# Spreading the tokens' inverse roots by two transfers through device memory instead of eight matmuls

## The reference

```python
def rms_norm(x, gain=None):
    y = x * lax.rsqrt(jnp.mean(x * x, axis=-1, keepdims=True) + EPS)
    ...
def modulate(h, shift, scale):
    return h * (1 + scale[:, None, :]) + shift[:, None, :]

for i in range(DEPTH):
    mod = cond @ mod_w[i] + mod_b[i]
    sh1, sc1, g1, sh2, sc2, g2, sh3, sc3, g3 = jnp.split(mod, 9, axis=-1)
    h = modulate(rms_norm(x), sh1, sc1)
    x = x + 0.5 * g1[:, None, :] * swiglu(h, ffn1_w_gu[i], ffn1_w_down[i])
    h = modulate(rms_norm(x), sh2, sc2)
    ...                                   # y = dsa_mixer(h) or fox_mixer(h)
    x = x + g2[:, None, :] * y
    h = modulate(rms_norm(x), sh3, sc3)
    x = x + 0.5 * g3[:, None, :] * swiglu(h, ffn2_w_gu[i], ffn2_w_down[i])
    x = rms_norm(x, post_gain[i])
```

## Time and profile before

| | |
|---|---|
| median of 3 runs | 2023.62 us (2021.04 to 2023.71) |
| the profiled execution | 2023.55 us, its span 2021.7 us |
| TensorE busy | 1986.2 us (98%), 9174 matmuls |
| VectorE busy | 1109.7 us (55%) |
| ScalarE busy | 726.7 us (36%) |
| GpSimd busy | 193.4 us (10%) |
| mean granted clock of TensorE | 0.993 |
| transfers | 253.97 MB, mean 126 GB/s |

### The profile page before, as it was taken

How to read it: one execution, slowest core, us unless ns; L and a number is a source line. 1 busy time by engine, 2 the same in 40 slices (tenths; PEclk the granted TensorE clock), 3 DMA queues, 4 the chain that set the end, 5 groups by cost and what they waited for, 6 DMA issues and landing times.

```text
span 2021.7 us, 23587 instructions
## 1 busy us (share of the span) xinstructions
PE 1986.2 (98%) x9174; PEld 1645.4 (81%) x9174; DVE 1109.7 (55%) x1705; ACT 726.7 (36%) x1066; POOL 193.4 (10%) x221
## 2 busy tenths in 40 slices
PE   6999999999999999999999999999999999999997
PEld 4888888888888888888888888877888888888886
DVE  7665553788757655636863553475454573333334
ACT  5222312554644222225322222345555442222223
POOL 3110000026600100000110100000000000000000
PEclk9999999999999999999999999999999999999998
DMA  8665542322025655623553632222221122323221
GB/s 318 239 214 180 184 156 88 100 87 74 22 98 194 216 172 194 189 77 108 188 190 104 205 125 83 94 84 64 73 72 54 63 94 104 104 83 108 81 87 57
DMA packets 72014, 253.97 MB, mean 126 GB/s; under 512 B 8025, under 2 KB 8153, under 8 KB 71938
## 3 DMA queue, kind: packets, MB, share of 16 engines
q1 hardware_dynamic: 53280, 185.62, 28.0%
q0 software_dynamic: 18512, 67.26, 10.0%
q10 hardware_dynamic: 146, 0.09, 0.0%
HBM read 250.70 MB, written 2.10 MB: 125 GB/s over the span
## 4 chain that ended last, share of the span: by engine, by line
PE 76%; issue 19%; DVE 3%; POOL 1%; ACT 1%; DMA 0%; POOLq 0%; SPq 0%; DVEq 0%; ACTq 0%
PE bank L1297 23%; PE bank L1302 23%; PE bank L1298 23%; PE bank L1762 1%; PE bank L1720 1%; PE bank L1361 1%; PE bank L1651 1%; PE bank L1493 1%; PE bank L1495 1%; DVE dve_tmp L876 1%; PE bank L1494 0%; PE bank L1708 0%; DVE wlo L751 0%; PE bank L1626 0%; DVE h_lo L869 0%
## 5 line engine op out<-in xcount | busy, mean ns | idle before, releaser
L1297 PE MATMUL bank<-h_hi,whi 128*128 128x512 f32 x1808 | 712.3, 394 | 6.8 <-DVE wlo L751 4.5
L1298 PE MATMUL bank<-h_hi,wlo 128*128 128x512 f32 x1808 | 706.1, 391 | 0.0
L1302 PE MATMUL bank<-h_lo,whi 128*128 128x512 f32 x1808 | 594.1, 390 | 0.5 <-POOL h_lo L331 0.5
L411 ACT ACTIVATE whi<-wraw 128x1024 fp32r<-128x1024 f32 x338 | 347.1, 1053 | 267.0 <-PE bank L1302 263.9
L751 DVE TENSOR_TENSOR wlo<-wraw,whi 128x1024 fp32r<-128x1024 f32 x324 | 389.2, 1223 | 57.3 <-ACT whi L411 56.5
L1297 PEld LDWEIGHTS bank<-h_hi,whi 128*128 128x128 f32 x1808 | 341.2, 189 | 79.3 <-issue 5.0
L1302 PEld LDWEIGHTS bank<-h_lo,whi 128*128 128x128 f32 x1808 | 340.5, 188 | 73.1 <-POOL h_lo L331 1.2
L1298 PEld LDWEIGHTS bank<-h_hi,wlo 128*128 128x128 f32 x1808 | 341.0, 189 | 68.6
L1297 PE MATMUL bank<-hid_hi,whi 128*128 128x512 f32 x832 | 324.3, 390 | 0.0
L1302 PE MATMUL bank<-hid_lo,whi 128*128 128x512 f32 x832 | 323.7, 389 | 0.0
L1298 PE MATMUL bank<-hid_hi,wlo 128*128 128x512 f32 x832 | 323.7, 389 | 0.0
(11 more groups left out here) (239 smaller groups left out, 1390.1 us busy)
## 6 DMA issues: line engine op xcount, KB each, us to landing
wraw<-in_w_units_dram SPq DMA_DIRECT2D x306, 512.0 KB, 3.5
arena<-in_mod_t_dram POOLq DMA_DIRECT2D x96, 512.0 KB, 4.9
mod_tile<-in_mod_t_dram POOLq DMA_DIRECT2D x32, 512.0 KB, 4.7
wraw<-in_w_units_dram SPq DMA_DIRECT2D x32, 384.0 KB, 3.4
arena<-in_mod_t_dram SPq DMA_DIRECT2D x12, 512.0 KB, 7.9
xT<-in_xt_dram SPq DMA_DIRECT2D x8, 256.0 KB, 4.5
out_dram<-xT SPq DMA_DIRECT2D x8, 256.0 KB, 2.3
mod_tile<-in_mod_t_dram SPq DMA_DIRECT2D x2, 512.0 KB, 9.5
```

The lines of the kernel that those rows point to most:

```text
L411: act.activation(whi[:, s % RING, :, :], wraw[:, s % RING, :, :], ACT.Copy).then_inc(hi_ready, 1)
L1297: pe.matmul(dst, whi[:, w, k, :], hi_, start=first, stop=False)
L1298: pe.matmul(dst, wlo[:, w, k, :], hi_, start=False, stop=False)
L1302: return pe.matmul(dst, whi[:, s % RING, k, :], lo_, start=False, stop=last)
```

## The change

In norms 1, 2, 5 and 6 the root no longer goes through TensorE and a bank. ScalarE issues a transfer of `rstd` (128 partitions x 4 numbers, 16 bytes each) to a row of 512 numbers in device memory, waits until it has landed, and issues a second one that reads this row for each of the 128 partitions into `ssum`. VectorE waits for the second. The row has the order of partition first and block second, so token b * 128 + p lies at place 4 p + b. The VectorE instructions that read `ssum` view it as 4 blocks of 128 numbers with a step of four (`from_row`), and their other operands as 4 blocks of 128 neighbours (`by_block`). The splits of the root and the eight matmuls go; the counts that other waits use (`ROOTS_BEFORE`, `rb_kept`, `rb_ready`, `root_ready`) follow.

```diff
+        BY_DMA = [1, 2, 5, 6]
+        def by_block(ap):
+            return ap.rearrange("q (b p) -> q b p", b=NB)
+        def from_row(ap):
+            return ap.rearrange("q (p b) -> q b p", b=NB)
...
+        norm_roots = nc.dram_tensor("norm_roots", (len(BY_DMA), SEQ), F32).ap()
...
             def round_h(st, s):
-                act.wait_ge(rb_ready, RB_BEFORE[v])
-                act.activation(ssum[:, :], bank[RB], ACT.Copy).then_inc(rb_kept, 1)
+                if st in BY_DMA:
+                    n, j = BY_DMA.index(st), NORM_JOB[st]
+                    act.wait_ge(rstd_ready, j + 1)
+                    act.dma_start(norm_roots[n, :].rearrange("(p b) -> p b", b=NB), rstd[:, j % 2, 0:NB])\
+                        .then_inc(norm_root_out, 16)
+                    act.wait_ge(norm_root_out, 16 * (n + 1))
+                    act.dma_start(ssum[:, :], norm_roots[n:n + 1, :].broadcast_to([P, SEQ])).then_inc(norm_root_in, 16)
...
             def spread_rstd(st):
                 if st in NORM:
                     lo(LAST_UNIT[st] - 1)
-                split_roots(j, NB)
-                if st in NORM:
                     lo(LAST_UNIT[st])
                 else:
-                    dve.wait_ge(rb_ready, st + 1)
+                    split_roots(j, NB)
+                    dve.wait_ge(rb_ready, 4 if st else 1)
...
             def early_ffn(s):
                 for q in range(2):
-                    dve.tensor_tensor(sq[:, q, :], bank[(s + q) % 4], ssum[:, :], ALU.mult).then_inc(evicted, 1)
+                    ...
+                        dve.tensor_tensor(by_block(sq[:, q, :]), by_block(bank[(s + q) % 4]), from_row(ssum[:, :]),
+                                          ALU.mult).then_inc(evicted, 1)
...
             def norm(st, s, take_early, late=False):
-                dve.wait_ge(rb_kept, v)
+                    dve.wait_ge(norm_root_in, 16 * (BY_DMA.index(st) + 1))
...
-                    dve.scalar_tensor_tensor(out=dve_tmp[:, k % 2, :], in0=xT[:, k, :], scalar=column[:, k:k + 1],
-                                             in1=ssum[:, :], op0=ALU.mult, op1=ALU.mult).then_inc(normed, 1)
+                        dve.scalar_tensor_tensor(out=by_block(dve_tmp[:, k % 2, :]), in0=by_block(xT[:, k, :]),
+                                                 scalar=column[:, k:k + 1], in1=from_row(ssum[:, :]), op0=ALU.mult,
+                                                 op1=ALU.mult).then_inc(normed, 1)
...
             def early(s, st):
-                        if q == 0 and k == 6 and st != 3:
-                            stat_spread(RB, ROOTS_BEFORE[st], NORM_JOB[st])
```

More of the change, by code:

```diff
@@ L225, in build @@
         gained, pool_posted = sem("gained"), sem("pool_posted")
+        norm_root_out, norm_root_in = sem("norm_root_out"), sem("norm_root_in")
         rows_done, rows_kept = sem("rows_done"), sem("rows_kept")
@@ L384, in _ @@
             job(18, 4)
-            pool.wait_ge(rb_kept, len(NORM) + 1)
+            pool.wait_ge(rb_kept, 2)
             pool.wait_ge(gained, KT)
@@ L393, in build @@
         POST_RB = 4
-        ROOTS_BEFORE = [0, 1, 3, 4, 5, 6, 15, 16]
+        ROOTS_BEFORE = {0: 0, 3: 2, 4: 3, 7: 12}
         LAST_UNIT = {st: down + KT + 3 for st, down in (
@@ L432, in round_h @@
                 v, sh, _ = modulation(st)
-                act.wait_ge(rb_ready, RB_BEFORE[v])
-                act.activation(ssum[:, :], bank[RB], ACT.Copy).then_inc(rb_kept, 1)
+                if st in BY_DMA:
[5 more added lines that the diff above has]
+                    act.dma_start(ssum[:, :], norm_roots[n:n + 1, :].broadcast_to([P, SEQ])).then_inc(norm_root_in, 16)
+                else:
+                    act.wait_ge(rb_ready, 2)
+                    act.activation(ssum[:, :], bank[RB], ACT.Copy).then_inc(rb_kept, 1)
                 for k in range(KT):
@@ L732, in _ @@
             ffn(3, 7)
-            act.wait_ge(rb_ready, 9)
+            act.wait_ge(rb_ready, 5)
             act.activation(ssum[:, :], bank[4], ACT.Copy).then_inc(rb_kept, 1)
@@ L842, in early_ffn @@
                 for q in range(2):
-                    dve.tensor_tensor(sq[:, q, :], bank[(s + q) % 4], ssum[:, :], ALU.mult).then_inc(evicted, 1)
+                    if s == FFN_BASE[2]:
+                        dve.tensor_tensor(sq[:, q, :], bank[(s + q) % 4], ssum[:, :], ALU.mult).then_inc(evicted, 1)
+                    else:
+                        dve.tensor_tensor(by_block(sq[:, q, :]), by_block(bank[(s + q) % 4]), from_row(ssum[:, :]),
+                                          ALU.mult).then_inc(evicted, 1)
             def early_dsa(s):
                 early_shift(s)
-                link(dve.tensor_tensor(sq[0:72, 0, :], bank[EARLY_BANK[1][0]][0:72, :], ssum[0:72, :], ALU.mult))
+                link(dve.tensor_tensor(by_block(sq[0:72, 0, :]), by_block(bank[EARLY_BANK[1][0]][0:72, :]),
+                                       from_row(ssum[0:72, :]), ALU.mult))
                 dve.tensor_scalar(ikx[0:72, :], sq[0:72, 0, :], shift_out[0:72, 0:1], None, ALU.add).then_inc(evicted, 1)
-                dve.tensor_tensor(sq[:, 1, :], bank[EARLY_BANK[1][1]], ssum[:, :], ALU.mult).then_inc(early_scaled, 1)
+                dve.tensor_tensor(by_block(sq[:, 1, :]), by_block(bank[EARLY_BANK[1][1]]), from_row(ssum[:, :]), ALU.mult)\
+                    .then_inc(early_scaled, 1)
             def early_fox(s):
                 early_shift(s)
-                link(dve.tensor_tensor(sq[0:HEADS, 0, :], bank[EARLY_BANK[4][0]][0:HEADS, :], ssum[0:HEADS, :], ALU.mult))
-                dve.tensor_tensor(sq[:, 1, :], bank[EARLY_BANK[4][1]], ssum[:, :], ALU.mult).then_inc(early_scaled, 1)
+                link(dve.tensor_tensor(by_block(sq[0:HEADS, 0, :]), by_block(bank[EARLY_BANK[4][0]][0:HEADS, :]),
+                                       from_row(ssum[0:HEADS, :]), ALU.mult))
+                dve.tensor_tensor(by_block(sq[:, 1, :]), by_block(bank[EARLY_BANK[4][1]]), from_row(ssum[:, :]), ALU.mult)\
+                    .then_inc(early_scaled, 1)
             def norm(st, s, take_early, late=False):
@@ L875, in norm @@
                         dve.wait_ge(h_ready, KT * v + k - 1)
-                    dve.scalar_tensor_tensor(out=dve_tmp[:, k % 2, :], in0=xT[:, k, :], scalar=column[:, k:k + 1],
-                                             in1=ssum[:, :], op0=ALU.mult, op1=ALU.mult).then_inc(normed, 1)
+                    if st in BY_DMA:
+                        dve.scalar_tensor_tensor(out=by_block(dve_tmp[:, k % 2, :]), in0=by_block(xT[:, k, :]),
+                                                 scalar=column[:, k:k + 1], in1=from_row(ssum[:, :]), op0=ALU.mult,
+                                                 op1=ALU.mult).then_inc(normed, 1)
+                    else:
+                        dve.scalar_tensor_tensor(out=dve_tmp[:, k % 2, :], in0=xT[:, k, :], scalar=column[:, k:k + 1],
+                                                 in1=ssum[:, :], op0=ALU.mult, op1=ALU.mult).then_inc(normed, 1)
                     if k == 1:
@@ L969, in ffn @@
                         if f == 2 and t == 0 and n == 1:
-                            dve.wait_ge(rb_ready, 5)
+                            dve.wait_ge(rb_ready, 3)
                         if f == 2 and t == 0 and 1 <= n <= 4:
@@ L1595, in _ @@
                 if j == 0:
-                    pe.wait_ge(root_ready, 3)
+                    pe.wait_ge(root_ready, 2)
                     for g in range(KV_HEADS):
```

4 lines of the change are left out of this document (2 added, 2 removed).

## The result

| | before | after |
|---|---|---|
| median of 5 runs, same chip | 2022.88 us (2020.42 to 2023.71) | 2055.59 us (2053.20 to 2056.73) |
| ratio, 95% interval | | 1.0162 [1.0148, 1.0176] |
| profiled span | 2021.7 us | 2053.7 us |
| mean granted clock | 0.993 | 0.986 |

The kernel became slower by 32.7 us, 1.6%. The forecast was 2037.

The account below looks back on a forecast made before the run. TensorE was taken to bound the kernel, with 76% of the chain. Late norm starts summed to 9.0 us, with the clock 13.4, stepped reads nothing: from 2023.55 to 2037 us, own range 2028 to 2052, 8-in-10 range 2028 to 2060.

Parts of the forecast that it names:

- Its structure: At four norms a late start meets TensorE: slack none at sites 1 and 3, shift columns' 1.0 us at 2 and 4.
- Part 2: Two transfers in series, 2.2 and 3.2 us, replace the 3.33 us path; 1.8 more at site 2; sum 9.0 us.
- d: Lateness of the norm start against before, from GpSimd's root to VectorE's norm: 2.3 us, 4.1 at site 2.
- Part 4: VectorE's reads in steps of four floats, ten instructions per site: no surcharge taken; 5.4 us per site at twice the time.
- Part 3: Low clock after TensorE's idle time at the shift columns: 3.4 us at site 2, 1.0 for the other three together.
- Rival B: Stepped reads lengthen VectorE's chain by 5.4 us at sites 1 and 3, 4.9 at 2 and 4: about 2055 us; chance 0.37.

Follow-up runs that it names:

- experiment 7: The changed kernel with only GpSimd's four loads at site 2 held until the second transfer has landed: 2049.47 us in one run.
- experiment 1: The kernel before, matmuls and copy kept, but the copy writes in the transfer's order and VectorE reads in steps: 2036.70 us, ratio 1.0076.
- experiments 3 and 4: Filler matmuls on TensorE ahead of the shift columns: 3 in the changed kernel, 2054.05 us; 4 with the row also read plainly, 2039.52 us.
- dma_plain: The changed kernel with both transfers, but VectorE reads the landed row without steps, so tokens get other tokens' roots: 2045.06 us, ratio 1.0113.
- experiment 9: The changed kernel with loads held and the second transfer reading 128 different rows of an input instead of one row 128 times: 2038.98 us, one run.
- hold: The changed kernel with SP's last two weight loads ahead of each norm and GpSimd's four at site 2 held until the row landed: 2041.26 us.

## Why the prediction was wrong

*Its structure held.* The eight matmuls of each site left TensorE's path with no gain (32 fewer of 9174), the wait appeared at the shift columns of all four sites, and sites 1 and 3 had no slack, 2 and 4 had VectorE's slack of 1.5. With the measured terms the same places give 32.4 of 33.0 us by VectorE's lane, 33.2 by the later lane.

*Part 2, the two legs, was mis-sized.* I took 2.2 + 3.2 us and, for site 2, 1.8 more. Measured are 2.8 to 4.1 and 3.3 to 3.8 at sites 1, 3 and 4, together 6.6 to 7.3, and 5.5 more at site 2 (experiment 7). The first leg's value was chosen by its size, 2 KB, from a row of 16 KB; the runs show that its time is made by what lies beside it, 1.4 us alone and 2.8 to 4.1 with the weight loads that I named only for the second leg. So d is 4.1, 8.9, 3.3, 3.5 instead of 2.3, 4.1, 2.3, 2.3, and the part's sum 4.1 + (8.9 - 1.0) + 3.3 + (3.5 - 1.0) = 17.8 instead of 9.0. For site 2 I halved the loads' own slow-down; the two transfers took three times my addition of 1.8. The 4.6 us for both, which the prediction gives by the Trainium skill (DMA: Bandwidth & Descriptors, Anatomy of one DMA), were lower still: even with the loads held they took 5.3 to 5.4. The first alone, at 1.4 us, came in below the fixed part of about 2.0 us; that section is on transfers that GpSimd issues, and these are ScalarE's.

*Part 4, the reading order, was a step set to nothing that costs 3.9 us a site.* I gave it no surcharge because no row had one, but all those rows read neighbouring elements, so they could not speak for steps. Alone it makes 15.4 us (experiment 1), 13.5 without the longer copy of that run.

*Part 3, the clock, was right in its place and wrong in its price.* Low spells came at all four sites, not only behind site 2, and cost next to nothing, because VectorE's lane was later or level at three of them (experiments 3 and 4). I had added a clock term to the shift; it belongs inside one lane, under a maximum. Under plain reads, as forecast, it was 5.5 us by the times. That this is near my 4.4 is in part luck: I had 3.4 at site 2 and 1.0 for the others together, and the stretches of dma_plain show 2.2 at site 2 and 4.7 at sites 1 and 4.

*Rival B's number came out for another reason.* It had 5.4 us a site for the steps and 9.0 for the transfers; measured are 3.9 and 17.8 by the same places. The steps by those places are 20.6 in B and 14.6 as measured. B's too large term, its too small one and the clock that it let in on top (0 to 4.4) cancel; that its number was met is luck. The forecast of parts 2 and 3 without the steps, +13.4, has its own test in dma_plain: +23.7. So 10.3 of the 19.3 us missed are the transfers' size, with some 1 us of clock in it, and the other 9.0 are what the steps add on top of it, both to some 3 us.

*Not settled:* how loads beside it make a transfer of 2 KB longer, which no run takes apart, why the legs of one site differ by over 1 us from run to run, and why the second leg keeps 3.5 to 3.9 us with nothing beside it, of which experiment 9 explains about 1.

## What to carry to other kernels

- A small transfer on the critical path is priced by what is in flight at that moment, not by its bytes. Look for the loads issued within a few us of it, by any engine: here the same 2 KB took 1.4, 2.8 to 4.1 or 6.9 us, and holding four loads back started the norm behind them 5.5 us earlier.
- A change of data layout is a cost on every instruction that reads it. If no row has the pattern, price it from both ends and measure it by one kernel that changes the pattern alone.
- Where two engines run side by side behind a late start, add the terms along each lane and take the later lane. A wait that shows on the busiest engine, and a low clock behind it, may have next to no price.

## What the runs showed of the hardware

- A two-operand VectorE instruction of 512 fp32 columns took 0.75 us, and 1.14 with one of its operands in steps of 16 bytes; with a bank as the other operand 0.69 and 1.06. ScalarE writing in such steps took 1.08 in place of 0.60.
- 2 KB from the tile to device memory: 128 pieces of 16 bytes 1.4 us, 512 pieces of 4 bytes 8.6 us, without other loads started beside them (medians of four; 2.0 us at one site).
- 256 KB into 128 partitions: 2.8 us from 128 rows (one run), 3.9 us from one row 128 times.
- The clock. In the changed kernel it was at the low level after every one of TensorE's waits at the columns, 3.9 to 9.6 us long. In experiment 1 a wait of 1.1 us stands in both kernels, with 0.50 behind it in one and 1.00 in the other. In hold, TensorE's waits at the columns, and the windows behind those of 2.8 us at site 1 and 2.7 at site 2:

```profile
PE bank L1441 <- DVE sq L917: 10.9, 4, 2.8
```
```profile
402.00:404.00 2.00, 0.82 (x5) 0.81 (x6) 1.97 (x4) 1.29 (x2) 0.00 (x0) 1.00 0.85 313
404.00:406.00 2.00, 2.00 (x10) 1.62 (x10) 1.96 (x3) 0.95 (x2) 0.00 (x0) 1.00 0.48 190
...
618.00:620.00 2.00, 2.00 (x6) 1.54 (x5) 1.96 (x4) 1.67 (x2) 0.00 (x0) 0.50 1.03 412
```

  It stayed at 1.00 behind the first and fell to 0.50 behind the second. The length of the wait alone doesn't tell, then, which level follows.
